# The hooks of the in2 stage placed some steps earlier in a two-block transformer kernel

## The reference

```python
def token_mixer(h, w_in, b_f, lb, g_o, w_out):
    z = h @ w_in                                  # 2048 -> 7176 columns
    ... q_a, k_a, v_a = z[:1024], z[1024:2048], z[2048:3072]; f_a = next 8 columns + b_f
    y_fox = forgetting_attention(q_a, k_a, v_a, f_a)      # 8 heads, decay from cumsum(log_sigmoid(f_a))
    q_b, f_b, i_b, g_b = four slices of 1024 columns
    log_f = logaddexp(log(lb), log1p(-lb) + log_sigmoid(f_b))
    k_b = (1 - lb) * sigmoid(-f_b)
    o_b = hgrn2_recurrence(q_b, k_b, i_b, log_f)          # 8 heads, chunks of 64 tokens
    o_b = rms_norm(o_b, g_o) * silu(g_b)
    return concatenate([y_fox, o_b]) @ w_out
```

## Time and profile before

| | |
|---|---|
| median of the runs | 2587.8 us (2586.45 to 2589.02, 3 runs) |
| profiled execution | 2587.8 us, its span 2586.0 us |
| TensorE matmul busy | 2490.8 us, 96% of the span |
| VectorE busy | 1483.3 us, 57% |
| ScalarE busy | 1228.7 us, 48% |
| DMA | 446.26 MB, mean 173 GB/s |
| steps of in2 with hooks | about 1300 to 1620 us of the span |

### The profile page before, as it was taken

How to read it: one execution, slowest core, us unless ns; L and a number is a source line. 1 busy time by engine, 2 the same in 40 slices (tenths; PEclk the granted TensorE clock), 3 DMA queues, 4 the chain that set the end, 5 groups by cost and what they waited for, 6 DMA issues and landing times.

```text
span 2586.0 us, 32619 instructions
## 1 busy us (share of the span) xinstructions
PE 2490.8 (96%) x11851; PEld 2070.2 (80%) x11851; DVE 1483.3 (57%) x1768; ACT 1228.7 (48%) x1535; POOL 47.0 (2%) x89
## 2 busy tenths in 40 slices
PE   7999868999999999999999999989999999999997
PEld 6788646888888888888798888878888888888876
DVE  4665675554445454444656756566666666644465
ACT  4554254444444444444564344455655555444454
POOL 1000400000000000000000000000000000000000
PEclk9999879999999999999999999999999999999999
DMA  6765102666666666555654545546565665655553
GB/s 225 236 183 164 42 1 86 188 189 190 187 190 189 188 187 209 189 191 191 183 170 137 147 145 171 187 147 188 185 188 182 188 184 180 203 198 195 194 169 134
DMA packets 232757, 446.26 MB, mean 173 GB/s; under 512 B 14016, under 2 KB 22932, under 8 KB 232148
## 3 DMA queue, kind: packets, MB, share of 16 engines
q1 hardware_dynamic: 230468, 435.10, 54.6%
q0 software_dynamic: 2192, 9.83, 1.2%
HBM read 442.78 MB, written 2.10 MB: 172 GB/s over the span
## 4 chain that ended last, share of the span: by engine, by line
PE 92%; DVE 4%; ACT 2%; DMA 1%; issue 1%; SPq 0%; DVEq 0%; ACTq 0%
PE pg L1871 28%; PE pg L1873 28%; PE pg L1872 28%; DMA raw<-w_in 1%; PE pt L2329 1%; DVE wlo L1118 1%; PE pt L1894 1%; PE pt L2169 1%; PE pt L1998 1%; ACT S L768 1%; PE pt L2118 0%; ACT whi L596 0%; DVE S L1427 0%; DVE AT L1430 0%; DVE H L1217 0%
## 5 line engine op out<-in xcount | busy, mean ns | idle before, releaser
L1118 DVE TENSOR_TENSOR wlo<-raw,whi 128x1024 fp32r<-128x1024 f32 (+2 forms) x836 | 1005.8, 1210 | 983.2 <-ACT whi L596 982.3
L596 ACT ACTIVATE whi<-raw 128x1024 fp32r<-128x1024 f32 (+2 forms) x836 | 870.7, 1044 | 1186.6 <-PE pg L1873 1151.5
L1871 PE MATMUL pg<-whi,AH 128*128 128x512 f32 (+2 forms) x2240 | 867.9, 387 | 13.8 <-DVE AL L1228 8.9
L1873 PE MATMUL pg<-whi,AL 128*128 128x512 f32 (+2 forms) x2240 | 860.5, 384 | 0.0
L1872 PE MATMUL pg<-wlo,AH 128*128 128x512 f32 (+2 forms) x2240 | 859.8, 384 | 0.0
L1871 PEld LDWEIGHTS pg<-whi,AH 128*128 128x128 f32 x2240 | 421.3, 188 | 97.5 <-DVE AL L1228 10.0
L1873 PEld LDWEIGHTS pg<-whi,AL 128*128 128x128 f32 x2240 | 421.1, 188 | 83.7
L1872 PEld LDWEIGHTS pg<-wlo,AH 128*128 128x128 f32 x2240 | 421.5, 188 | 80.3
L1871 PE MATMUL pg<-whi,FH 128*128 128x512 f32 x704 | 274.4, 390 | 0.0
L1873 PE MATMUL pg<-whi,FL 128*128 128x512 f32 x704 | 273.9, 389 | 0.0
L1872 PE MATMUL pg<-wlo,FH 128*128 128x512 f32 x704 | 273.9, 389 | 0.0
(11 more groups left out here) (400 smaller groups left out, 1646.9 us busy)
## 6 DMA issues: line engine op xcount, KB each, us to landing
raw<-w_up SPq DMA_DIRECT2D x264, 512.0 KB, 4.1
raw<-w_in SPq DMA_DIRECT2D x176, 512.0 KB, 3.7
raw<-w_down SPq DMA_DIRECT2D x176, 512.0 KB, 3.6
raw<-w_gate SPq DMA_DIRECT2D x88, 512.0 KB, 3.6
raw<-w_out SPq DMA_DIRECT2D x64, 512.0 KB, 3.6
raw<-w_ple_gate SPq DMA_DIRECT2D x32, 512.0 KB, 4.0
raw<-w_in SPq DMA_DIRECT2D x16, 288.0 KB, 3.0
raw<-w_in SPq DMA_DIRECT2D x16, 260.0 KB, 2.9
```

The costliest lines, as they stand in the source:

```text
L596: A(whi[:, n % RING, 0:w], raw[:, n % RING, 0:w], ACT.Copy).then_inc(hi_ready, 1)
L1118: V.tensor_tensor(wlo[:, n % RING, 0:w], raw[:, n % RING, 0:w], whi[:, n % RING, 0:w].bitcast(F32), ALU.subtract).then_inc(lo_ready, 1)
L1871: mm(o, xh, wh, start=first and k == 0, stop=False)
L1873: ins = mm(o, xl, wh, start=False, stop=last and k == SK - 1)
```

## The change

The hooks of in2 on TensorE, ScalarE and VectorE go to other steps, most of them one to four earlier. `lv_start` begins at 46 instead of 48, `fox_start` at 93 instead of 96. Relative to `lv_start(l)`, `lv_times` and `lv_differ(l + 1)` and `lv_take` stay at 0, 1 and 3; `lv_level` goes from 2 to 1, `lv_decay(l + 1)` from 3 to 2, `lv_copy` from 4 to 3. `mix2(2)` and `mix2(3)` go one index earlier in out2's tables of ScalarE and VectorE. The tensors after `Z2` (`HQ`, `HKT`, `QF`, `KF2`, `OHF` and others) begin right behind it and no more on a multiple of 512 bytes: `Z2` takes 57408 bytes, which was rounded up to 57856.

```diff
-        o_y = (o_b + NT * D_IN2 * 4 + 511) // 512 * 512
+        o_y = o_b + NT * D_IN2 * 4
...
 # ScalarE
-                       (2, 5): ..., (2, 7): hgrn_log, (4, 2): hgrn_sums, (5, 4): hgrn_q,
-                       (6, 5): fox_log, (5, 3): lambda: lv_decay(0), (5, 6): lambda: lv_decay(1),
-                       (10, 2): fox_q, (11, 1): fox_sums, (11, 5): ho_squares, (11, 7): ho_root,
-                       (14, 2): lambda: hg_gate(0), (14, 5): mix2(0), (14, 7): mix2(1)}
+                       (2, 5): ..., (2, 7): hgrn_log, (4, 2): hgrn_sums, (5, 2): hgrn_q,
+                       (5, 4): fox_log, (5, 0): lambda: lv_decay(0), (5, 3): lambda: lv_decay(1),
+                       (9, 7): fox_q, (10, 4): fox_sums, (11, 2): ho_squares, (11, 4): ho_root,
+                       (14, 2): lambda: hg_gate(0), (14, 4): mix2(0), (14, 6): mix2(1)}
...
-                    between[at_step(lv_start(l) + 3)] = lambda l=l: lv_decay(l + 1)
+                    between[at_step(lv_start(l) + 2)] = lambda l=l: lv_decay(l + 1)
-                    between[at_step(lv_start(l) + 4)] = lambda l=l: lv_copy(l)
+                    between[at_step(lv_start(l) + 3)] = lambda l=l: lv_copy(l)
...
-            between = {1: lambda: hg_gate(1), 4: mix2(2), 6: mix2(3)}
+            between = {1: lambda: hg_gate(1), 3: mix2(2), 5: mix2(3)}
...
 # VectorE
-                       (3, 1): hgrn_min, (3, 4): hgrn_logf, (4, 6): hgrn_k, (5, 1): lambda: lv_differ(0), (5, 3): lambda: lv_differ(1),
-                       (5, 4): fox_abs, (5, 7): lv_diagonal, (6, 6): fox_log,
-                       (10, 5): fox_k, (11, 5): ho_gain, (11, 6): ho_sums, (12, 1): ho_norm,
-                       (14, 3): lambda: hg_times(0), (14, 5): mix2(0), (14, 7): mix2(1)}
+                       (3, 1): hgrn_min, (3, 4): hgrn_logf, (4, 5): hgrn_k, (4, 7): lambda: lv_differ(0), (5, 1): lambda: lv_differ(1),
+                       (5, 3): fox_abs, (5, 5): lambda: (fox_log(), lv_diagonal()),
+                       (10, 1): fox_k, (11, 2): ho_gain, (11, 3): ho_sums, (11, 6): ho_norm,
+                       (14, 3): lambda: hg_times(0), (14, 4): mix2(0), (14, 6): mix2(1)}
...
-            between = {2: lambda: hg_times(1), 4: mix2(2), 6: mix2(3)}
+            between = {2: lambda: hg_times(1), 3: mix2(2), 5: mix2(3)}
...
 # TensorE
-            hooks = {(4, 1): hgrn_sums, (4, 5): hgrn_k, (5, 3): hgrn_q, (5, 6): lv_diagonal,
-                     (10, 1): fox_q, (10, 4): fox_k, (10, 7): lambda: fox_sums(0), (11, 0): lambda: fox_sums(4), (11, 4): hgrn_out,
-                     (14, 4): lambda: fox_turn(0), (14, 6): lambda: fox_turn(1)}
-            hooks.update({at_step(lv_start(l) + 2): lambda l=l: lv_level(l) for l in range(8)})
+            hooks = {(4, 1): hgrn_sums, (4, 4): hgrn_k, (5, 1): hgrn_q, (5, 4): lv_diagonal,
+                     (9, 6): fox_q, (10, 0): fox_k, (10, 2): lambda: fox_sums(0), (10, 3): lambda: fox_sums(4), (11, 1): hgrn_out,
+                     (14, 3): lambda: fox_turn(0), (14, 5): lambda: fox_turn(1)}
+            hooks.update({at_step(lv_start(l) + 1): lambda l=l: lv_level(l) for l in range(8)})
...
-    return 48 + 4 * l
+    return 46 + 4 * l
...
-    return 96 + 2 * u
+    return 93 + 2 * u
```

More of the change, by code:

```diff
@@ L1020, in _ @@
                        (2, 1): hgrn_sig, (2, 3): lambda: link(A(tmp, f, ACT.Abs)),
-                       (2, 5): lambda: link(A(tmp, tmp, ACT.Exp, scale=-1.0)), (2, 7): hgrn_log, (4, 2): hgrn_sums, (5, 4): hgrn_q,
-                       (6, 5): fox_log, (5, 3): lambda: lv_decay(0), (5, 6): lambda: lv_decay(1),
-                       (10, 2): fox_q, (11, 1): fox_sums, (11, 5): ho_squares, (11, 7): ho_root,
-                       (14, 2): lambda: hg_gate(0), (14, 5): mix2(0), (14, 7): mix2(1)}
+                       (2, 5): lambda: link(A(tmp, tmp, ACT.Exp, scale=-1.0)), (2, 7): hgrn_log, (4, 2): hgrn_sums, (5, 2): hgrn_q,
+                       (5, 4): fox_log, (5, 0): lambda: lv_decay(0), (5, 3): lambda: lv_decay(1),
+                       (9, 7): fox_q, (10, 4): fox_sums, (11, 2): ho_squares, (11, 4): ho_root,
+                       (14, 2): lambda: hg_gate(0), (14, 4): mix2(0), (14, 6): mix2(1)}
             for l in range(8):
                 if 2 <= l + 1 < 8:
-                    between[at_step(lv_start(l) + 3)] = lambda l=l: lv_decay(l + 1)
+                    between[at_step(lv_start(l) + 2)] = lambda l=l: lv_decay(l + 1)
                 if l < 3:
-                    between[at_step(lv_start(l) + 4)] = lambda l=l: lv_copy(l)
+                    between[at_step(lv_start(l) + 3)] = lambda l=l: lv_copy(l)
             between.update({at_step(fox_start(u) + 1): lambda u=u: fox(u) for u in range(10)})
```

## The result

The changed kernel takes 2648.5 us (median of 4 runs, 2646.4 to 2651.0) against 2588.4 us of the kernel before on the same chip: ratio 1.0233, 95% interval 1.0216 to 1.0251, 60 us slower. The forecast was slower, 2623 us with a range of 2611 to 2642: the direction held, the size didn't, and the range missed by 6.5 us.

A forecast was written before the change was run, and what follows sets the result against it. TensorE, at work 96% of the span, was taken as the bound. Waits 28.8 us plus restarts 1.8 less old waits 2.2 gave 28.4; with clock 6.8, 35.2 on 2587.8: 2623 us, range 2611 to 2642.

The forecast's parts named there:

- The waits: TensorE's waits in in2 at hgrn_q, the levels, the fox hooks and evacuations: 28.8 us, less 2.2 of old waits.
- Levels: TensorE's level matmuls wait for VectorE's lv_times at each level: five times 2.05 us, level 2 2.7, level 7 about 3.5.
- three evacuation waits: hgrn_out and the fox units at 97 and 105 wait for a chunk's evacuation: 0.3 us each, 1.0 with wake-up.
- Rival (c): Level wait paid once, as VectorE and ScalarE gain the missing step and keep it: 2599 us, chance 0.05.
- Rival (d): Not slower: lv_times ends before TensorE asks, and the 2.2 us of old waits go: 2585.6 us, chance 0.04.
- TensorE's clock: After the four longest waits TensorE falls to 1.2 GHz, 1.7 us lost each, 6.8 us; none after the shorter waits.
- rival (b): Every wait of about 2 us drops TensorE's clock: 2635 us, or 2663 with slow level matmuls; chance 0.29.
- (a): Rival: TensorE's waits cost only their own length, nothing for the clock: 2616 us, chance 0.24.
- Cold restarts: Held TensorE work runs slower: 0.8 us for three newly held levels, 1.0 us for seven other hooks.
- hgrn_k: TensorE's hgrn_k, now before step 36, isn't late, as ScalarE's copy ends at 1327.31, before 1327.65: no cost.
- the mix hooks: Mix hooks one step earlier keep their distances or have over 10 us of cover in out2: no cost.
- The offset: HQ and its neighbours 448 bytes lower: no effect, as lv_times lasts 1217 to 1231 ns on both LG buffers.

The follow-up runs named there:

- levels_only: The kernel before with only TensorE's lv_level one step earlier (lv_start + 1): 2636.1 us, ratio 1.0177.
- wait_apart: The kernel before with TensorE waiting for lv_times at lv_start + 1, level matmuls still at lv_start + 2: 2618.3 us, ratio 1.0111.
- levels_back: The changed kernel with TensorE's lv_level put back to lv_start + 2, all else changed: 2601.6 us, ratio 1.0054 against the kernel before.
- q_mended: levels_back with VectorE's lv_differ(0) moved behind the evacuation that hgrn_q waits for: 2598.6 us, ratio 1.0031 against the kernel before.
- offset_only: The kernel before with only HQ and the tensors behind it 448 bytes lower: 2594.5 us, ratio 1.0010.
- levels_filled: levels_only plus eight extra 512-column TensorE matmuls ahead of each level's wait for lv_times: 2620.8 us, ratio 1.0127 against the kernel before.

## Why the prediction was right and wrong

- **The waits: right, nearly one by one.** Levels 16.4 us (10.3 + 2.7 + 3.5 = 16.5 forecast), level 0 2.9 (3.0), hgrn_q 4.0 (4.0), fox_q 2.3 (2.1), fox_k 0.4 (0.3), fox_sums 2.0 (1.9). Only the three evacuation waits are larger, 2.3 for 1.0. The one of the fox unit at step 97 is 1.2 us, and it is VectorE's evacuation after all, which comes late (timeline of the changed kernel):

```profile
1598.72 0.74 DVE L1152 TENSOR_SCALAR Z<-pg,SM 128x512 f32<-128x512 f32 x1
1599.57 1.10 PE L2254 MATMUL pt<-KF,QF 128*128 128x256 f32 x4 [1.22 <-issue]
```

  Ahead of it VectorE did the end of ho_norm (L1682, 2.29 us from 1592.67) and four operations of a fox unit (1596.14 to 1597.68); the prediction took its earliest turn. Sum 30.3 for 28.8. The distance from level 4 to level 5, where the clock stayed up, is 17.1 us for 16.8 forecast; from level 3 to 4, with one fall, it is 20.0.
- **The level wait recurs** (step *Levels*): right. Rival (c), paid once, would have left one wait; there are eight. Rival (d) is out for the same reason.
- **The step that failed: TensorE's clock.** I took a fall of 3.4 us, 1.7 us of loss, behind the four longest waits and none behind the seven of about 2 us: 6.8 us. It measured some 28 us. Both parts were wrong. Waits of 2 us do drop the clock when a level's matmuls follow (levels_only: eight of eight waits of 2.0 to 4.1 us). And a fall there lasts 6.8 or 10.2 us rather than the 3.4 of the row that I took it from the earlier trace rows; that row had wide matmuls behind it. wait_apart has the same idle times and 10 us lost for 29, so what stands behind the wait makes most of the difference. The trace of before had a long fall too, behind the 1.91 us wait of the earlier trace rows with TensorE busy throughout, of which the earlier trace rows show one microsecond (its windows):

```profile
309.00:319.00 10.00, 10.00 (x50) 10.00 (x50) 7.77 (x20) 0.85 (x2) 2.34 (x1) 0.50 0.00 0
```

  The bound of 5.2 us a level that I kept as rival (b)'s far end was the true size of the longest falls (5.1 us); I should have asked what stands behind each wait before giving it the price of another one. Rival (b), 2635 to 2663 us, is what happened, with 0.29; (a), nothing for the clock, is out. Even so two waits (level 0, 2.9 us, and level 4, 2.02) had no fall in that execution, and the order of length didn't decide which.
- **Cold restarts.** In levels_back levels 1 to 6 all take 3.52 us; in before levels 2, 4, 6 and 7 took 3.77 to 3.79, although only level 2 shows idle time. The weight loads (PEld) tell why. In before, level 3's begin during the last wide matmul, level 7's only when VectorE's lv_times is done:

```profile
1411.69 1.09 PEld L2329 LDWEIGHTS pt<-Z 128*128 128x128 f32 x8
```

```profile
1470.55 0.63 PEld L2329 LDWEIGHTS pt<-Z 128*128 128x128 f32 x5 [0.45 <-DVE Z L1641]
```

  The Trainium skill, "TensorE: Matmul & The Clock Gate", in its opening table, says that the queue pulls weight loads ahead of matmuls in flight. That agrees with these two rows, and a held first load costs the level 0.27 us. Of the other restarts three can be read: fox_q and fox_k take 1.94 us in levels_back for 1.75 in before, and so does hgrn_q in q_mended, 0.19 us where I took 0.15. The rest weren't separated.
- **hgrn_k, the mix hooks, the DMA at nothing:** no wait of TensorE stands before them. **The offset at nothing:** right for lv_times and the in2 stretch, wrong for out2, where it costs 1.3 us (offset_only).

## What to carry to other kernels

In an order written by hand, count the distance between an operand and its use in the slowest engine's steps, including the splits that must go first on the engine that makes it: here the distance of two steps (5.46 us) covered 4.73 us, and one step could not. On a kernel that TensorE bounds, price a wait as its length plus the clock that falls behind it, and take that price from a row with the same kind of work behind it; if a wait can't be avoided, put it in front of wide matmuls (18 us less here, levels_only against wait_apart). Price a moved buffer over all its readers, TensorE's matmuls too.

## What the runs showed of the hardware

- The same wait of 2.02 us before level 1 left the clock at 1.00 with a wide step behind it (wait_apart), and was followed by 10.2 us at 1.2 GHz with the level's 64-column matmuls behind it (changed kernel). The eight falls of 6.8 or 10.2 us in levels_only became five in wait_apart, four of 3.4 us and one of 6.8 behind level 0.
- An idle time of only 0.93 us (levels_filled) was followed by a fall, one of 0.90 us was and another was not, and in the changed kernel one of 2.92 us was not. The length of the idle time alone doesn't tell.
- In five of the falls in the changed kernel TensorE was busy without a gap and yet at 1.2 GHz for 6.8 us or more: a busy share of 100% in the windows says nothing of the speed, PEclk beside it does.
- With `OHF` and `OLF` 448 bytes lower, at a start that is no multiple of 512, out2's 192 matmuls on them take 1.2 to 1.3 us longer in all five kernels that have it; those on `OHG` and `OLG` beside them don't.
